# Where three groups of transfers stand in a decoder trunk on one core: the sums of the down weights in gate and up, the loads at the border, the transposes of the last product

## The chip, the cores and the metric

The kernel runs on one core of a Trainium2 chip. Its metric is the time of one execution on the device in microseconds, taken as the median of several runs. TensorE (PE in the rows; PEld is its weight load) multiplies, VectorE (DVE), ScalarE (ACT) and GpSimd (POOL) work on elements, and SyncE (SP) issues most of the transfers, which 16 DMA engines carry out. SP and POOL each feed a queue of their own to the same 16 engines.

## The reference

The program is a decoder trunk of two layers on 1024 tokens of width 1024, all in float32.

```python
for i in range(DEPTH):                       # DEPTH = 2
    h = rmsnorm(x, norm_mix[i])
    x = x + (even_mixer(...) if i % 2 == 0 else odd_mixer(...))
    h = rmsnorm(x, norm_ffn[i])
    x = x + conv_ffn(h, w_gate[i], w_up[i], conv_w[i], conv_b[i], w_down[i])
    gate = jax.nn.sigmoid(rmsnorm(x, norm_ple[i]) @ w_ple_gate[i])
    x = x + gate * (p[i] @ w_ple_proj[i])

def conv_ffn(h, w_gate, w_up, conv_w, conv_b, w_down):
    g = causal_dwconv(h @ w_gate, conv_w, conv_b)
    return (jax.nn.gelu(g) * (h @ w_up)) @ w_down     # D_FF = 2816
```

The even mixer projects h to queries, keys and values of two groups of heads; in one group each query keeps the 256 keys with the highest score of an indexer. The odd mixer is a dilated window attention.

## The kernel before

**Stages.** Each layer is a row of stages, and each stage has an instruction list of its own for every engine: input projection, attention, output projection, gate and up with the down pass (`ffn_stage`), and the gated embedding. Every float32 factor is split in a high and a low part (`w_hi`, `w_lo`), and a product is three matmuls (`mm3`, lines 78 to 80): ScalarE rounds the high part, GpSimd or VectorE subtracts it for the low part, and TensorE multiplies.

**Input projection of layer 0** (`project_select_stage`, names `l0in_` and `l0h_`). Six strips of 512 columns, each of 8 token tiles. While TensorE is in strip s, four chunks (512 KB each) of strip s + 1 are loaded by SP into `l0h_raw` (L1987), split by ScalarE (L2021) and by GpSimd (L2080). In ScalarE's list chunk c stands ahead of the two token tiles 2c and 2c + 1 that it copies out of PSUM, and SP stores these two tiles ahead of its next load. All along VectorE finds each query's threshold by 31 rounds of bisection (L2162 to L2172) and then makes the mask tile by tile (L2182 to L2189); ScalarE's count for the first of these tiles (L2050) stands in its list behind its work on the next-to-last strip. Layer 1 has the simpler `projection_stage` (`l1in_`, `k_raw`, `k_w_lo`).

**The sums.** The down projection is done by seven products of half size (`DOWN`), r = 0 to 6; three of them (r = 2, 3, 6) have a sum of two blocks of `w_down` on the right. Class `RightSums` makes these sums in device memory, by transfers alone: six copies of 1408 KB (`copy`, L2263), then six transfers of the same size that add onto what is there (`add`, L2269). They are issued by GpSimd, and the program before has them in the input projection of each layer: copies beside strips 1 and 2, adding transfers beside strips 3 and 4.

**Gate and up** (`ffn_stage`, names `l0ff_`, `l1ff_`). NG = 11 groups of W = 14 steps; a step is 12 matmuls on one of 14 factors of a group, with `q` the number of the step over all groups and `n` its number in the group. The weights of a group come in two loads of 1024 KB, `raw_g` and `raw_u` (L830), which SP issues at n = 8 and 9 once the buffers' last use is over; a ring of six slots `w_hi`, `w_lo` holds split factors ahead of TensorE. `Q` is the number of all steps.

**Down pass.** Seven products of 11 steps each, z = 11r + k. A step multiplies a left factor (from `a11`, `a12`, `a22`, read back from `acts`, in the rows `l0ff_a`) with a right one (`d_one`, and for a difference `d_two`), both split three steps ahead: `split_right` and `split_left` on ScalarE, `sum_left`, `sum_right`, `low_right`, `low_left` on VectorE. `load_down(z)` loads the right factor. In step z VectorE also adds one tile of the product before to `x` (`add`, L2804), which is reloaded from `kept`. During the last product `nfeed.turn` transposes the first two normed token tiles of the next stage (L188) in banks of `bank_u`; product 5 stands in these banks until VectorE has added it. Turn 0 takes banks 0 and 1, turn 1 banks 2 and 3, and product 5's eight adds go through banks 0 to 3 twice.

## Time and profile before

| | |
|---|---|
| median of 3 runs | 3159.48 us (3158.32 to 3169.77) |
| the profiled execution, its own time | 3161.22 us |
| its span in the profile | 3159.2 us |
| TensorE busy | 3014.0 us, 95% of the span |
| VectorE busy | 2271.2 us, 72% |
| ScalarE, GpSimd busy | 1444.3 us (46%), 1403.9 us (44%) |
| mean DMA rate | 110 GB/s |

The difference of 2.0 us between time and span lies ahead of and behind the profiled instructions. Layer 0's input projection lies at 226 to 517 us of the span, its gate and up at 945 to 1355, its down pass at 1355 to 1591; the stages of layer 1 that the text speaks of are at 1714 to 1990, 2392 to 2802 and 2802 to 3037. TensorE's clock is given as a share of its full 2.4 GHz: 1.00 is that, 0.50 is 1.2 GHz.

### The profile page before, as it was taken

The page shows a single profiled execution, that of the slowest core. Times are in us where ns is not written, and L with a number is a line of the kernel's source. Part 1 is how long each engine was busy: PE and PEld are TensorE (multiplying, and loading weights), DVE is VectorE, ACT ScalarE, POOL GpSimd, SP SyncE. Part 2 cuts the span into 40 slices and gives each one's busy share as a digit, 9 for nine tenths or more (in the row PEclk, how much of TensorE's full clock was granted, in tenths as well). Part 3 has the DMA queues.
Part 4 walks back from the last instruction along what each step waited for, and adds up shares of the span by engine and source line. Part 5 has one row for each costly group of instructions (what it writes and reads, how often), then busy time and mean ns, then how long its engine had stood idle before and what let it go on. Part 6 is the DMA issues. An engine that isn't in the chain of part 4 may idle for free. (4 is left out here: it accounts for less than half of the span.)

```text
span 3159.2 us, 44227 instructions
## 1 busy us (share of the span) xinstructions
PE 3014.0 (95%) x14830; PEld 2520.0 (80%) x14830; DVE 2271.2 (72%) x3459; ACT 1444.3 (46%) x3125; POOL 1403.9 (44%) x905
## 2 busy tenths in 40 slices
PE   7999889999999999999899999999998999999989
PEld 6777777989877888878788788899886888878877
DVE  6599957879458887779943332799648888779952
ACT  4384435878343343334432211688633333434431
POOL 3105445366235655523422455677315566533330
PEclk9999999999999999999999999999999999999999
DMA  5325574223312222365311585323121222265411
GB/s 179 122 61 164 140 181 122 60 54 78 116 54 80 80 84 82 127 246 193 99 61 37 195 178 170 81 66 80 54 88 54 96 82 80 81 240 197 157 48 53
DMA packets 288086, 349.07 MB, mean 110 GB/s; under 512 B 88316, under 2 KB 181292, under 8 KB 287916
## 3 DMA queue, kind: packets, MB, share of 16 engines
q1 hardware_dynamic: 274860, 312.27, 30.9%
q0 software_dynamic: 13056, 34.60, 4.9%
q8 instruction: 98, 1.61, 0.2%
q14 instruction: 72, 0.59, 0.1%
HBM read 268.70 MB, written 112.20 MB: 121 GB/s over the span
## 5 line engine op out<-in xcount | busy, mean ns | idle before, releaser
L2162 DVE TENSOR_SCALAR_CACHE_REDUCE k_x<-k_x,l0in_cand,l0in_want 128x384 bf16<-128x384 f32 (+1 forms) x186 | 175.0, 1004 | 1.2 <-DVE l0in_before L2157 0.2
L78 PE MATMUL l1in_acc<-k_w_lo,k_hi 128*128 128x512 f32 x384 | 151.7, 395 | 5.2 <-POOL k_w_lo L681 2.7
L2648 POOL TENSOR_TENSOR l1ff_w_lo<-l1ff_raw_g,l1ff_w_hi 128x512 fp32r<-128x512 f32 x64 | 93.5, 1466 | 138.6 <-ACT l1ff_w_hi L2511 138.5
L2648 POOL TENSOR_TENSOR l0ff_w_lo<-l0ff_raw_g,l0ff_w_hi 128x512 fp32r<-128x512 f32 x64 | 91.9, 1438 | 140.8 <-ACT l0ff_w_hi L2511 140.7
L2540 ACT ACTIVATE k_x<-k_x 128x512 f32<-128x512 f32 x88 | 55.7, 633 | 212.3 <-DVE k_x L2742 212.3
L79 PE MATMUL l1in_acc<-k_w_hi,k_lo 128*128 128x512 f32 x384 | 150.8, 393 | 0.0
L80 PE MATMUL l1in_acc<-k_w_hi,k_hi 128*128 128x512 f32 x384 | 150.6, 392 | 0.0
L725 DVE TENSOR_TENSOR l1in_sq<-l1in_out 128x512 f32<-128x512 f32 x32 | 40.4, 1264 | 114.7 <-ACT l1in_out L658 114.0
L1619 DVE TENSOR_TENSOR l1dil_pt_lo<-l1dil_ring,l1dil_pt_hi 128x512 fp32r<-128x512 f32 x192 | 101.9, 553 | 4.6 <-ACT l1dil_pt_hi L1555 2.3
L1635 DVE CUSTOM_DVE_ANT_0 l1dil_s<-l1dil_s,l1mix_sliding 128x128 f32<-128x128 f32 (+7 forms) x128 | 97.3, 761 | 9.0 <-PE l1dil_s L1719 4.7
L1555 ACT ACTIVATE l1dil_pt_hi<-l1dil_ring 128x512 fp32r<-128x512 f32 x192 | 92.5, 492 | 22.6 <-PE l1dil_ring L1702 21.4
L2652 POOL TENSOR_TENSOR l0ff_s_lo<-l0ff_s_tmp,l0ff_s_hi 128x512 fp32r<-128x512 f32 x31 | 47.8, 1543 | 101.2 <-ACT l0ff_s_hi L2557 101.2
L2652 POOL TENSOR_TENSOR l1ff_s_lo<-l1ff_s_tmp,l1ff_s_hi 128x512 fp32r<-128x512 f32 x31 | 48.0, 1551 | 99.7 <-ACT l1ff_s_hi L2557 99.7
L78 PEld LDWEIGHTS l1in_acc<-k_w_lo,k_hi 128*128 128x128 f32 x384 | 72.7, 189 | 21.4 <-POOL k_w_lo L681 3.6
L681 POOL TENSOR_TENSOR k_w_lo<-k_raw,k_w_hi 128x1024 fp32r<-128x1024 f32 x20 | 48.7, 2435 | 87.3 <-ACT k_w_hi L646 87.3
L1896 DVE SCALAR_TENSOR_TENSOR k_x<-l0h_r,l0h_wi,k_x 128x384 f32<-128x384 f32 (+2 forms) x96 | 83.2, 957 | 5.8 <-ACT l0h_r L1881 5.8
L80 PEld LDWEIGHTS l1in_acc<-k_w_hi,k_hi 128*128 128x128 f32 x384 | 72.9, 190 | 15.5
L79 PEld LDWEIGHTS l1in_acc<-k_w_hi,k_lo 128*128 128x128 f32 x384 | 73.0, 190 | 14.9
L2790 DVE TENSOR_TENSOR l0ff_d_lo<-l0ff_d_one,l0ff_d_hi 128x512 fp32r<-128x512 f32 x77 | 66.5, 864 | 18.4 <-ACT l0ff_d_hi L2566 18.3
L2790 DVE TENSOR_TENSOR l1ff_d_lo<-l1ff_d_one,l1ff_d_hi 128x512 fp32r<-128x512 f32 x77 | 66.3, 862 | 17.8 <-ACT l1ff_d_hi L2566 17.4
L2698 DVE TENSOR_TENSOR l1ff_w_lo<-l1ff_raw_u,l1ff_w_hi 128x512 fp32r<-128x512 f32 x65 | 52.4, 806 | 35.8 <-ACT l1ff_w_hi L2511 35.8
L2566 ACT ACTIVATE l1ff_d_hi<-l1ff_d_one 128x512 fp32r<-128x512 f32 x77 | 48.1, 625 | 65.2 <-DVE l1ff_d_one L2786 38.6
(647 smaller groups left out, 11304.4 us busy)
## 6 DMA issues: line engine op xcount, KB each, us to landing
l_right_sums<-in_w_down POOLq DMA_DIRECT2D x24, 1408.0 KB, 14.0
acts<-k_x SPq DMA_DIRECT2D x88, 256.0 KB, 2.0
k_raw<-in_w_in_odd SPq DMA_DIRECT2D x24, 512.0 KB, 4.9
l0ff_raw_g<-in_w_gate SPq DMA_DIRECT2D x11, 1024.0 KB, 5.2
l0ff_raw_u<-in_w_up SPq DMA_DIRECT2D x11, 1024.0 KB, 5.6
l0ff_a<-acts SPq DMA_DIRECT2D x44, 256.0 KB, 5.3
l0ff_d_one<-in_w_down SPq DMA_DIRECT2D x44, 256.0 KB, 2.8
l1ff_raw_g<-in_w_gate SPq DMA_DIRECT2D x11, 1024.0 KB, 5.2
```

The lines of the kernel that those rows point to most:

```text
L78: pe.matmul(out, a_hi, b_lo, start=start, stop=False)
L79: pe.matmul(out, a_lo, b_hi, start=False, stop=False)
L80: return pe.matmul(out, a_hi, b_hi, start=False, stop=stop)
L1555: act.activation(pt_hi[:, slot, c:512], ring[:, bank, c:512], ACT.Copy).then_inc(rounded, 1)
L1619: dve.tensor_tensor(pt_lo[:, slot, c:512], ring[:, bank, c:512], pt_hi[:, slot, c:512].bitcast(F32), ALU.subtract).then_inc(drained, 1)
L1635: dve.tensor_tensor_reduce(s, s, crow[:, b, 0:(t + 1) * P] if FOX else masks[t], -SCALE, 1e38, ALU.add, ALU.min, nmax[:, i:i + 1]).then_in ...
L1896: dve.scalar_tensor_tensor(cols, r[:, (t - T0) % NB, 0:(t + 1) * P], wi[:, t, bass.ds(h, 1)], cols, ALU.mult, ALU.add).then_inc(acc_done, 1)
L2162: tick(dve.tensor_scalar(hits[:, cols], score[:, cols], cand[:, i:i + 1].bitcast(F32), want[:, i:i + 1], ALU.is_ge, ALU.add, accum_out=exc ...
L2540: act.activation(a[n % 2], c[n % 2], ACT.Gelu_apprx_tanh).then_inc(gelu_done, 1)
L2648: pool.tensor_tensor(buf.ring_lo[q % R][:], operand(q), buf.ring_hi[q % R][:].bitcast(F32), ALU.subtract).then_inc(w_lo_done[0], 1)
L2652: pool.tensor_tensor(s_lo[z % DEEP][:], left(z), s_hi[z % DEEP][:].bitcast(F32), ALU.subtract).then_inc(s_lo_done[0], 1)
L2790: dve.tensor_tensor(d_lo[z % DEEP][:], d_raw[z % DEEP][0][:], d_hi[z % DEEP][:].bitcast(F32), ALU.subtract).then_inc(d_lo_done, 1)
```

## The change

Three edits, each in both layers.

1. The six copies and six adding transfers leave the input projections. They are issued by GpSimd in gate and up, one at n = 6 and one at n = 13: the copies in groups 0 to 2, the adding ones in groups 3 to 5.
2. At the border from gate and up to the down pass, SP's list has another order. Four loads of `a11` and `a12` go out at step Q - 1, ahead of the last stores; the right factor z = 7 goes ahead of the remaining ones; the loads of `a22` and of `x` follow one at a time behind the right factors z = 8 to 20.
3. `nfeed.turn` stands behind steps 7 and 9 of the last product instead of 6 and 8. The first turn waits for all but two of product 5's adds, the second one for all.

```diff
@@ projection_stage, gpsimd
-                    if s in (1, 2) and c < right_sums.count // 2:
-                        right_sums.copy(pool, (s - 1) * (right_sums.count // 2) + c)
-                    if s in (3, 4) and c < right_sums.count // 2:
-                        right_sums.add(pool, (s - 3) * (right_sums.count // 2) + c)
@@ project_select_stage, gpsimd
-                    if s == 1 and t < right_sums.count:
-                        right_sums.copy(pool, t)
-                    if s == 3 and t < right_sums.count:
-                        right_sums.add(pool, t)
@@ ffn_stage, sync, in the loop over q
+                if q == Q - 1:
+                    sp.wait_ge(filled, Q - 2)
+                    load_part(a11, (0, 0), range(8, 11), a11_in)
+                    load_part(a12, (0, 1), range(8, 9), a12_in[1])
@@ ffn_stage, sync, behind that loop
-            sp.wait_ge(filled, Q - 2)
-            load_part(a11, (0, 0), range(8, 11), a11_in)
-            load_part(a12, (0, 1), range(8, 9), a12_in[1])
-            sp.wait_ge(stored[0], 16 * 2 * NG)
-            load_part(a12, (0, 1), range(9, 11), a12_in[2])
-            sp.wait_ge(filled, Q)
-            load_part(a22, (1, 1), range(4, 8), a22_in)
-            sp.wait_ge(stored[1], 16 * 2 * NG)
             for z in range(DEEP + 3, Z):
                 r, k = divmod(z, KB2)
                 load_down(z)
-                if (r, k) in ((0, 7), (0, 9)):
-                    t = k - 7
-                    for u in (t, t + 1):
-                        sp.dma_start(x[:, u, :], buf.kept[u * P:(u + 1) * P, :]).then_inc(x_in[0], 16)
-                if (r, k) == (0, 10):
-                    load_part(a22, (1, 1), range(8, 11), a22_in)
-                if r == 1 and k in (1, 4, 6, 8):
-                    t = {1: 4, 4: 5, 6: 6, 8: 7}[k]
-                    sp.dma_start(x[:, t, :], buf.kept[t * P:(t + 1) * P, :]).then_inc(x_in[1], 16)
+                if (r, k) == (0, 7):
+                    sp.wait_ge(stored[0], 16 * 2 * NG)
+                    load_part(a12, (0, 1), range(9, 11), a12_in[2])
+                    sp.wait_ge(stored[1], 16 * 2 * NG)
+                    sp.wait_ge(filled, Q)
+                if 8 <= z <= 11 or z in (14, 16, 18, 20):
+                    t = z - 8 if z <= 11 else z // 2 - 3
+                    sp.dma_start(x[:, t, :], buf.kept[t * P:(t + 1) * P, :]).then_inc(x_in[t // 4], 16)
+                if 9 <= z <= 11 or z in (13, 15, 17, 19):
+                    i = z - 5 if z <= 11 else z // 2 + 1
+                    load_part(a22, (1, 1), range(i, i + 1), a22_in)
@@ ffn_stage, gpsimd
+                if n in (6, 13) and grp < 6:
+                    i = 2 * (grp % 3) + (n == 13)
+                    right_sums.copy(pool, i) if grp < 3 else right_sums.add(pool, i)
@@ ffn_stage, tensor, down(z)
-                if r == len(DOWN) - 1 and k in (6, 8):
-                    if k == 6:
-                        pe.wait_ge(added, ADDED[r])
-                    nfeed.turn(pe, (k - 6) // 2)
+                if r == len(DOWN) - 1 and k in (7, 9):
+                    pe.wait_ge(added, ADDED[r] - 2 if k == 7 else ADDED[r])
+                    nfeed.turn(pe, (k - 7) // 2)
```

GpSimd's list in layer 0's input projection, beside strip 1, had these rows before: the low part of a chunk, two copies, the work on the statistics of two token tiles, and the next chunk.

```order
L2080 TENSOR_TENSOR l0h_w_lo<-l0h_raw,l0h_w_hi 128x1024
L2263 DMA l_right_sums<-in_w_down 704x512 x2
L2085 TENSOR_SCALAR k_stats<-k_stats 128x2x8
L2087 TENSOR_TENSOR k_stats<-k_stats,l0in_half 128x2x8
L2080 TENSOR_TENSOR l0h_w_lo<-l0h_raw,l0h_w_hi 128x1024
```

GpSimd's list of the changed kernel, in the first group of gate and up from n = 5 on (low parts for the ring, sums of weights, copies; its lines are numbered some 10 lower):

```order
L2638 TENSOR_TENSOR l0ff_w_lo_8910<-l0ff_raw_g,l0ff_w_hi_8904 128x512
L2255 DMA l_right_sums<-in_w_down 704x512
L2638 TENSOR_TENSOR l0ff_w_lo_8906<-l0ff_raw_g,l0ff_w_hi_8900 128x512
L2638 TENSOR_TENSOR l0ff_w_lo_8908<-l0ff_raw_g,l0ff_w_hi_8902 128x512
L2638 TENSOR_TENSOR l0ff_w_lo_8910<-l0ff_raw_g,l0ff_w_hi_8904 128x512
L2623 TENSOR_TENSOR k_x<-l0ff_raw_g 128x512
L2623 TENSOR_TENSOR k_x<-l0ff_raw_u 128x512
L2638 TENSOR_TENSOR l0ff_w_lo_8906<-k_x,l0ff_w_hi_8900 128x512
L2626 TENSOR_TENSOR l0ff_raw_g<-l0ff_raw_g 128x4x128
L2255 DMA l_right_sums<-in_w_down 704x512
```

A copy now stands between two low parts, the second of which is the last use of `raw_g` in the group, and another one among the sums for the next group.

SP's list at the border before, from the last store of gate and up on: ten loads of left factors stand ahead of the right factor of z = 7 (the row of L2278).

```order
L2413 DMA acts<-k_x 128x512
L2423 DMA l0ff_a_9895<-acts 128x512
L2423 DMA l0ff_a_9896<-acts 128x512
L2423 DMA l0ff_a_9897<-acts 128x512
L2423 DMA l0ff_a_9906<-acts 128x512
L2423 DMA l0ff_a_9907<-acts 128x512
L2423 DMA l0ff_a_9908<-acts 128x512
L2423 DMA l0ff_a_9913<-acts 128x512
L2423 DMA l0ff_a_9914<-acts 128x512
L2423 DMA l0ff_a_9915<-acts 128x512
L2423 DMA l0ff_a_9916<-acts 128x512
L2278 DMA l0ff_d_one_9880<-in_w_down 128x512
```

The same place of the changed kernel, from the last store on:

```order
L2405 DMA acts<-k_x 128x512
L2270 DMA l0ff_d_one_9862<-in_w_down 128x512
L2415 DMA l0ff_a_9889<-acts 128x512
L2415 DMA l0ff_a_9890<-acts 128x512
L2270 DMA l0ff_d_one_9859<-in_w_down 128x512
L2471 DMA k_x<-kept 128x1024
L2270 DMA l0ff_d_one_9860<-in_w_down 128x512
L2471 DMA k_x<-kept 128x1024
L2415 DMA l0ff_a_9895<-acts 128x512
L2270 DMA l0ff_d_one_9861<-in_w_down 128x512
L2471 DMA k_x<-kept 128x1024
L2415 DMA l0ff_a_9896<-acts 128x512
```

The right factor of z = 7 is now first behind the store, and those of z = 8, 9 and 10 each have a load of `x` or two behind them.

TensorE's list at the first turn before: the last matmuls of step 6 (slot 9873 of the right factor), the transposes, the first matmuls of step 7 (slot 9874).

```order
L80 MATMUL l0ff_bank_g<-l0ff_d_hi_9869,l0ff_s_hi_9861 128x512
L188 MATMUL l0ff_bank_u<-k_square,l0pg_xn 128x128 x8
L78 MATMUL l0ff_bank_g<-l0ff_d_lo_9874,l0ff_s_hi_9862 128x512
L79 MATMUL l0ff_bank_g<-l0ff_d_hi_9870,l0ff_s_lo_9866 128x512
L80 MATMUL l0ff_bank_g<-l0ff_d_hi_9870,l0ff_s_hi_9862 128x512
```

The same turn in the changed kernel, between steps 7 and 8, so one step (12 matmuls) later:

```order
L80 MATMUL l0ff_bank_g<-l0ff_d_hi_9852,l0ff_s_hi_9844 128x512
L188 MATMUL l0ff_bank_u<-k_square,l0pg_xn 128x128 x8
L78 MATMUL l0ff_bank_g<-l0ff_d_lo_9857,l0ff_s_hi_9845 128x512
L79 MATMUL l0ff_bank_g<-l0ff_d_hi_9853,l0ff_s_lo_9849 128x512
L80 MATMUL l0ff_bank_g<-l0ff_d_hi_9853,l0ff_s_hi_9845 128x512
```

The transposes are the same eight matmuls; only their place has moved.

## Rows read from the trace of the kernel before

**Rows 1.** The page, part 1: busy time, share of the span, instructions
```profile
PE 3014.0 (95%) x14830; PEld 2520.0 (80%) x14830; DVE 2271.2 (72%) x3459; ACT 1444.3 (46%) x3125; POOL 1403.9 (44%) x905
```

**Rows 2.** TensorE's waits, whole span: for whom, us in total, times, longest
```profile
PE l0w_t L78 <- POOL l0h_w_lo L2080: 18.5, 2, 13.3
...
PE l0ff_bank_u L188 <- DVE k_x L2804: 8.5, 1, 8.5
PE l1ff_bank_u L188 <- DVE k_x L2804: 8.1, 1, 8.1
PE l0ff_bank_g L78 <- DVE l0ff_s_lo L2808: 5.5, 1, 5.5
PE l1ff_bank_g L78 <- DVE l1ff_s_lo L2808: 5.4, 1, 5.4
...
PE l0w_t L78 <- POOL l0in_w_lo L2080: 4.2, 1, 4.2
...
PE l1in_acc L78 <- POOL k_w_lo L681: 2.7, 1, 2.7
```

**Rows 3.** Landing of the loads into l0h_raw (L1987), layer 0's input projection
```profile
DMA to landing us min/median/max: 3.6/4.9/13.5
```

**Rows 4.** Windows: PE, PEld, DVE, ACT, POOL busy; granted clock, DMA share, GB/s
```profile
333.00:376.00 43.00, 43.00 (x191) 35.52 (x190) 42.27 (x99) 22.41 (x142) 22.09 (x12) 1.00 0.33 98
416.00:428.00 12.00, 6.79 (x20) 5.10 (x19) 11.90 (x23) 5.32 (x35) 5.45 (x3) 0.72 1.12 231
468.00:480.00 12.00, 7.77 (x23) 5.82 (x22) 6.46 (x9) 5.20 (x11) 6.40 (x4) 0.72 0.29 115
```

**Rows 5.** Timeline of PE, 326 to 333 us: start, length, [wait before it]
```profile
326.88 0.80 PE L78 MATMUL l0w_t<-l0h_w_lo,l0h_hi 128*128 128x512 f32 x1 [13.27 <-POOL l0h_w_lo L2080]
...
332.16 0.45 PE L78 MATMUL l0w_t<-l0h_w_lo,l0h_hi 128*128 128x512 f32 x1
```

**Rows 6.** Timeline of DVE, 440 to 513 us: the mask tiles
```profile
473.32 0.15 DVE L2186 TENSOR_SCALAR l0in_cnt<-l0in_cnt 128x1 f32<-128x1 f32 x1 [31.34 <-ACT k_x L2050]
...
511.45 1.23 DVE L2189 SCALAR_TENSOR_TENSOR k_x<-k_x 128x1024 f32<-128x1024 f32 x1
```

**Rows 7.** GpSimd's DMA queue, 270 to 330 us: packets, MB, share of 16 engines
```profile
q0 software_dynamic: 2208, 8.65, 46.8%
```

**Rows 8.** The same queue, 375 to 440 us
```profile
q0 software_dynamic: 4320, 8.65, 75.1%
```

**Rows 9.** Line L2269, adding transfers: time to issue on POOL, ns min/median/max
```profile
L2269 POOL DMA_DIRECT2D l_right_sums<-in_w_down x12: 1105/1183/1607, 378.4 to 1895.6; - x12
```

**Rows 10.** Timelines of SP, ACT and PE around one group of gate and up
```profile
1034.69 0.38 SPq L830 DMA_DIRECT2D l0ff_raw_g<-in_w_gate  x1
...
1041.11 0.63 ACT L2511 ACTIVATE l0ff_w_hi<-l0ff_raw_g 128x512 fp32r<-128x512 f32 x1 [6.59 <-DMA l0ff_raw_g<-in_w_gate]
...
1055.39 0.39 PE L78 MATMUL l0ff_bank_g<-l0ff_lo,l0ff_w_hi 128*128 128x512 f32 x1
```

**Rows 11.** Timelines of SP, ACT and PE at the border of layer 0
```profile
1368.04 4.79 SPq L2423 DMA_DIRECT2D l0ff_a<-acts  x10
1372.93 0.49 SPq L2278 DMA_DIRECT2D l0ff_d_one<-in_w_down  x1
...
1379.84 0.63 ACT L2566 ACTIVATE l0ff_d_hi<-l0ff_d_one 128x512 fp32r<-128x512 f32 x1 [9.72 <-DMA l0ff_d_one<-in_w_down]
...
1381.89 0.77 PE L78 MATMUL l0ff_bank_g<-l0ff_d_lo,l0ff_s_hi 128*128 128x512 f32 x1 [5.52 <-DVE l0ff_s_lo L2808]
```

**Rows 12.** A window at that border, columns as in rows 4
```profile
1376.30:1387.10 10.80, 5.28 (x14) 4.14 (x14) 5.15 (x7) 3.56 (x7) 1.27 (x1) 0.68 1.04 403
```

**Rows 13.** Timelines of DVE and PE in layer 0's last product
```profile
1569.63 0.68 DVE L2804 TENSOR_TENSOR k_x<-k_x,l0ff_bank_u 128x512 f32<-128x512 f32 x1
...
1573.96 1.97 PE L188 MATMUL l0ff_bank_u<-k_square,l0pg_xn 128*128 128x128 f32 x8 [8.53 <-DVE k_x L2804]
1575.58 0.78 PE L78 MATMUL l0ff_bank_g<-l0ff_d_lo,l0ff_s_hi 128*128 128x512 f32 x1
```

More of the change, by code:

```diff
@@ L582, in load, with projection_stage @@
                      .rearrange("(k p) n -> p k n", p=P)).then_inc(arrived, 16)
-def projection_stage(nc, name, right_sums, x, buf, ident, proj, vsplit, vstored, stats, next_head=None):
+def projection_stage(nc, name, x, buf, ident, proj, vsplit, vstored, stats, next_head=None):
     S = len(buf.strips)
@@ L1930, in _, with project_select_stage @@
             first.begin(pe, hi, lo)
-def project_select_stage(nc, name, right_sums, hi, lo, strips, proj, vsplit, vstored, room, stats, score, mask, tail, square, decay, first, next_head=None):
+def project_select_stage(nc, name, hi, lo, strips, proj, vsplit, vstored, room, stats, score, mask, tail, square, decay, first, next_head=None):
     S = len(strips)
@@ L3006, in trunk @@
                                           EXTRA_AT + 9 * KB)
-                            project_select_stage(nc, L + "in", right_sums[layer], hi, lo, [w[:, c:c + 512] for c in HEADS_SRC], proj, vsplit, vstored, room, stats,
+                            project_select_stage(nc, L + "in", hi, lo, [w[:, c:c + 512] for c in HEADS_SRC], proj, vsplit, vstored, room, stats,
                                                  score, mask, tail, square, decay, first, fox)
@@ L3011, in trunk @@
                                   second_at=MERGED_AT + 8 * KB)
-                    projection_stage(nc, L + "in", right_sums[layer], x, heads, ident, proj, vsplit, vstored, stats, dil)
+                    projection_stage(nc, L + "in", x, heads, ident, proj, vsplit, vstored, stats, dil)
                 recycle(nc)
```

## The prediction

> **What bounds the kernel now.** I read the busy times first: TensorE works through 95% of the span [rows 1], and the change leaves its matmuls alone. So only its waits can be won or lost, and the list of waits comes next [rows 2]. The reader is to see three places. In layer 0's input projection TensorE waits 18.5 us in two pieces for low parts that GpSimd makes, and 4.2 us once more in a later strip (layer 1: 2.7). At each border to the down pass it waits 5.5 and 5.4 us for `s_lo`. At the first transposes of the next stage it waits 8.5 and 8.1 us for VectorE's last add of product 5. These waits sum to 52.9 us. Then I read timelines around each place for what was late, and windows for the granted clock, because a wait has a second price: after the 13.27 us wait at 326.88 the next 12 matmuls take 332.16 - 326.88 = 5.28 us [rows 5], where 12 of the clean window take 12 x 43.00 / 191 = 2.70 us [rows 4]. I count 2.6 us of slow clock behind a long wait. The windows behind the other waits of the stage stand at 0.72 [rows 4], so each of them has such a tail.
>
> **Edit 1, what it removes.** Beside copies and adding transfers a chunk's load takes up to 13.5 us to land, against a median of 4.9 and a best of 3.6 [rows 3]. In the clean window TensorE is busy in all of its 43.00 us at a DMA share of 0.33 [rows 4]: without transfers this stage has no wait of its own. So both waits for `l0h_w_lo` go, the 4.2 us one of the later strip too, since the same chain of load, split and low part stands behind it. That is 18.5 + 4.2 = 22.7 us, and three tails of 2.6 make 7.8: 30.5 us. VectorE could take the bound instead. It stands idle for 31.34 us before 473.32, waiting for ScalarE's count, which is queued behind ScalarE's copies out of PSUM and so moves forward with TensorE; then it works without a pause to 511.45 + 1.23 = 512.68 [rows 6]. If ScalarE comes 30.5 us earlier, the idle time is used up to the last microsecond, and VectorE ends at 512.7 - 30.5 = 482, about level with TensorE. I take 30; the bounds are 15 (VectorE or ScalarE keeps half of it) and 31. Layer 1 gives 2.7 us and a shorter tail: the wait is a fifth of the long one, and I take 1.7 us, so 4.4 (bounds 0 and 5.3).
>
> **Edit 1, what it adds.** The same twelve transfers per layer move the same bytes in another stage. Their cost for the 16 engines: six copies take 46.8% of 60 us, 4.7 us each [rows 7]; six adding ones 75.1% of 65 us, 8.1 us each [rows 8]. GpSimd is held 1.1 to 1.6 us for the issue of one [rows 9]. I do not have the copies' issue in a row and take the same for them. In gate and up the thing that can be late is the next group's weights. In one group `raw_g` is issued at 1034.69, ScalarE splits it at 1041.11, having waited 6.59 us for it, and TensorE uses it first at 1055.39 [rows 10]. From a split to the matmul the border takes 1381.89 - 1379.84 = 2.05 us [rows 11], so the factor is ready at 1043.2, 12.2 us early. That is the cover. The transfer at n = 6 is issued two to three steps, of 2.7 us, ahead of these loads, so it meets them; the one at n = 13 is done long before the next ones. Delay, worked out in two ways: the adding transfer's whole 8.1 us and its issue of 1.6 us, 9.7 us; or the worst stretching of rows 3, 13.5 / 4.9 = 2.8 times the 6.4 us of landing here, 11.3 us more. Both stay under 12.2, so I take nothing lost in gate and up. The margin of the second is small, and if the cover is gone, each of the 12 meetings (six groups, two layers) costs its excess and a tail of 2.6. A gain is excluded: TensorE does not wait there now.
>
> The Trainium skill, "DMA: Bandwidth & Descriptors", section "Queues, rings and completion order", has each DMA engine take its queues in turn, packet by packet. By that rule a load beside one transfer lasts at most about twice as long, some 6.4 us more, and the sum is the same. Rows 3 stretch further than that, with several transfers in flight. The same skill, "SBUF — State Buffer", section "SBUF: two separate sides", speaks against the change: VectorE in its fast modes can keep GpSimd from writing descriptors. That would hold GpSimd's low parts as well. The issue times of rows 9 show no hold beyond 1.6 us, and half of them were measured with VectorE all but saturated, as it is in the clean window (42.27 of 43.00 us [rows 4]); should the hold be longer in gate and up, it would act as the first rival below does.
>
> **Edit 2.** The first matmul of the down pass waits for the right factor of z = 7: its load is issued at 1372.93, behind ten loads that take the queue from 1368.04 for 4.79 us, ScalarE splits it at 1379.84, and TensorE goes on at 1381.89 after 5.52 us [rows 11]. In the new order it is issued at about 1368.1. With the same 6.9 us to its split it comes at 1375.0, and TensorE could go at 1377.0; it is ready at 1381.89 - 5.52 = 1376.4. So 0 to 0.7 us are left. Gain per layer: 5.5 and a tail of 2.6, less up to 0.7, so 7.5; two layers 15 (bounds 5 and 16). The four loads moved ahead of the stores go out in the last step of gate and up; SP has nothing else to send between them. What is late next is product 1's loads: each step now moves a right pair of 512 KB with 512 KB of `x` or 256 KB of `a22`, on average 896 KB (917,500 bytes) in 2.7 us, 340 GB/s. The border itself moved 403 GB/s at a share of 1.04 [rows 12]. It fits, with a sixth to spare.
>
> **Edit 3.** The first turn stood behind step 6, whose matmuls ended at 1573.96 - 8.53 = 1565.43, and waited until 1573.96 for the last of product 5's eight adds. The sixth, the last one that it will wait for now, ends at 1569.63 + 0.68 = 1570.3 [rows 13]. The turn also stands a step later: TensorE ends step 7 at 1565.4 + 2.7 = 1568.15 and waits until 1570.3, 2.15 us. Behind step 9, at 1573.6 + 2.0 or later, the second turn finds all adds done or misses them by a little. Before, 8.53 us and a tail of some 2 us were lost (one matmul takes 0.78 us behind the turn [rows 13], where one in the clean flow of rows 10 takes 0.39). After, 2.15 and a tail of at most 1.7. Gain 7.5 us in layer 0 and 7 in layer 1, 14.5 (bounds 8 and 19). The norm of the other token tiles and the next stage's start keep their place.
>
> **The sum.** 30 + 4.4 + 15 + 14.5 = 63.9 us. From the profiled execution's own 3161.2 us that is 3097.3; this execution is 1.7 us above the median of the three runs, less than the sum is worth. I say 3097.
>
> **The rivals.**
> *The transfers hold gate and up's weights back (the other side).* Place: the loads of `raw_g` and `raw_u` in groups 0 to 5. For it: the 13.5 us landing, and a load here is twice a chunk. Against it: only one transfer is in flight at n = 6, not several. It decides from 63.9 / 12 = 5.3 us lost at each meeting, 2.7 of wait and 2.6 of tail, so from a delay of 12.2 + 2.7 = 14.9 us. With a delay of 20 us it costs (7.8 + 2.6) x 12 = 125 us: 3222. In a mild form (delays of 13 to 14 us at the six adding meetings) it costs 6 x 4 = 24: 3121. Chance 0.04 for the strong form, 0.10 for the mild.
> *VectorE or ScalarE becomes the bound of the select stage.* For it: the idle 31.34 us are exactly what the gain uses, and VectorE works through all of the 39 us behind. Then edit 1 gives 15 instead of 30: 3112. Chance 0.12.
> *The border's stall comes back in product 1.* For it: the share of 1.04, with loads of `x` in between the right factors. Edit 2 then gives 5 instead of 15: 3107. Chance 0.11. To this belongs that the order at the border does nothing, since z = 7 lands late with its neighbours whatever stands ahead: also near 3107.
> My forecast, 3085 to 3104, has the remaining 0.63.
>
> **How the numbers follow.** A measurement of this kernel tells 0.5%, 15.8 us, from no change. The forecast and the second and third rival are all faster by more than that, as is most of the mild form: 0.91. Its rest and cases between the mild and the strong form give 0.05 for the same, the strong form 0.04 for slower. All terms at their upper bounds give 31 + 5 + 16 + 19 = 71 us, 3090, and half as much again as the tails I count (six of 2.6) could be hidden in rows that I did not sum, so the range begins at 3083. It ends at 3124, just beyond the mild form at 3121; outside lie the strong form and mixtures of two rivals.
>
> **What the changed profile would show.** Edit 1: no waits of `l0w_t` for `l0h_w_lo`, landings of `l0h_raw` under 7 us, the stage over at about 487 instead of 517, `right_sums` rows in gate and up, landings of `raw_g` longer at groups 0 to 5 and TensorE without a wait there. Wrong, if L78 or L80 wait for `l0ff_w_lo` or `w_hi` in these groups, or if the stage ends with VectorE alone at work. Edit 2: `d_one` of z = 7 issued right behind the last store, the wait under 1 us; wrong, if waits for `d_lo` or `s_lo` stand in product 1. Edit 3: the turn's wait at 2 us; wrong, if a second one stands at the next turn.

## The result and the profile after

The changed kernel takes 3167.74 us (median of 20 runs, 3161.39 to 3172.52), the kernel before 3157.74 us (20 runs beside them): ratio 1.0029, 95% interval 1.0022 to 1.0037. The forecast was 3097 us with a range of 3083 to 3124. The time lies outside it and is slightly longer than before.

TensorE's work is the same ([rows 1] for before); the page of the changed kernel:

```profile
PE 3018.5 (95%) x14830; PEld 2517.2 (79%) x14830; DVE 2285.1 (72%) x3459; ACT 1438.9 (45%) x3125; POOL 1385.1 (44%) x905
```

Its list of TensorE's waits answers to [rows 2]. Every wait that was to go is gone. `l0w_t` no longer waits for `l0h_w_lo`, the border's wait for `s_lo` is no longer near 5 us, and the turn's is 2.0 us in both layers (one sign of edit 2 being wrong shows faintly: a wait of 1.9 us for a left factor's low part, `s_lo` by GpSimd, in layer 1's product 1). In their place stand waits of gate and up, for low parts made by VectorE (L2691) and by GpSimd (L2638):

```profile
PE l0ff_bank_u L78 <- DVE l0ff_w_lo L2691: 20.1, 6, 4.2
PE l1ff_bank_u L78 <- DVE l1ff_w_lo L2691: 17.6, 6, 4.2
...
PE l0ff_bank_g L78 <- POOL l0ff_w_lo L2638: 6.5, 3, 2.9
...
PE l1ff_bank_g L78 <- POOL l1ff_w_lo L2638: 4.7, 3, 2.8
```

To see where the time is, I laid the first and last starts of each stage's matmuls side by side. One pair of rows for layer 0's gate and up, the kernel before and then the changed one (durations in ns, then first and last start in us):

```profile
L78 PE MATMUL l0ff_bank_g<-l0ff_lo,l0ff_w_hi x176: 389/389/775, 916.3 to 1345.7; 128*128 128x512 f32 x176
L78 PE MATMUL l0ff_bank_u<-l0ff_t_lo,l0ff_w_hi x132: 389/389/527, 947.6 to 1353.9; 128*128 128x512 f32 x132
```

```profile
L78 PE MATMUL l0ff_bank_g<-l0ff_lo,l0ff_w_hi x176: 389/389/775, 881.4 to 1346.9; 128*128 128x512 f32 x176
L78 PE MATMUL l0ff_bank_u<-l0ff_t_lo,l0ff_w_hi x132: 389/389/515, 912.8 to 1355.1; 128*128 128x512 f32 x132
```

The stage begins 34.9 us earlier and ends 1.2 us later. (Its first matmul is at 916.3 in the kernel before, not at the 945 given for this stage further up; in layer 1 it is at 2363.6. All distances here count from there.) The whole account in one profiled execution of each (us):

| stage | predicted | measured |
|---|---|---|
| input projection, layer 0 | -30 | -32.0 |
| input projection, layer 1 | -4.4 | -4.6 |
| border and turn, layers 0 and 1 | -29.5 | -12.4 and -6.6 |
| gate and up, layers 0 and 1 | 0 | +36.0 and +32.0 |
| elsewhere | 0 | -3.8 |
| span | -63.9 | +8.6 |

The windows say the same from the other side: mean clock and DMA share of gate and up in both layers, before and then after (columns as in [rows 4]). The DMA share rises from 0.26 to 0.42, and the stretch is longer by 36 and 31 us for the same matmuls.

```profile
916.00:1355.00 439.00, 427.46 (x1864) 352.04 (x1863) 354.10 (x379) 171.68 (x276) 252.48 (x168) 0.98 0.26 89
2363.00:2802.00 439.00, 427.40 (x1866) 352.32 (x1865) 357.11 (x379) 170.65 (x276) 255.71 (x168) 0.98 0.26 89
```

```profile
881.00:1356.00 475.00, 438.12 (x1864) 357.30 (x1862) 363.96 (x379) 168.45 (x276) 254.79 (x180) 0.96 0.42 121
2347.00:2817.00 470.00, 438.84 (x1859) 357.98 (x1857) 362.00 (x375) 166.43 (x273) 254.43 (x179) 0.96 0.42 122
```

**Two things happen in a group with transfers.** First, at n = 6. The timelines of GpSimd, SP, ScalarE and TensorE in layer 0's fifth group of the changed kernel:

```profile
1094.05 1.10 POOL L2261 DMA_DIRECT2D l_right_sums<-in_w_down  x1
...
1096.49 0.38 SPq L826 DMA_DIRECT2D l0ff_raw_g<-in_w_gate  x1
...
1109.14 0.63 ACT L2501 ACTIVATE l0ff_w_hi<-l0ff_raw_g 128x512 fp32r<-128x512 f32 x1 [14.84 <-DMA l0ff_raw_g<-in_w_gate]
...
1111.16 0.50 PE L78 MATMUL l0ff_bank_g<-l0ff_lo,l0ff_w_hi 128*128 128x512 f32 x1 [2.08 <-POOL l0ff_w_lo L2638]
```

The load is issued 2.4 us behind the adding transfer and takes 12.7 us to its split; in the kernel before it takes 5.1 to 5.4, and 6.4 once in each layer. In group 0 the transfer goes out 6.7 us ahead of the load, which then takes 5.7 us: so each layer has five meetings of a transfer with the loads, two with a copy and three with an adding transfer, not six. TensorE uses the factor as soon as it is ready, 2.08 us late. Second, at n = 13, the same group, GpSimd, VectorE and TensorE:

```profile
1122.57 1.11 POOL L2261 DMA_DIRECT2D l_right_sums<-in_w_down  x1
1123.29 1.71 POOL L2630 TENSOR_TENSOR l0ff_raw_g<-k_x,l0ff_raw_g 128x512 f32<-128x512 f32 x1
...
1127.00 1.64 POOL L2630 TENSOR_TENSOR l0ff_raw_u<-k_x,l0ff_raw_u 128x512 f32<-128x512 f32 x1
...
1123.10 6.11 DVE L2691 TENSOR_TENSOR l0ff_w_lo<-k_x,l0ff_w_hi 128x512 fp32r<-128x512 f32 x1
...
1129.26 0.50 PE L78 MATMUL l0ff_bank_u<-l0ff_lo,l0ff_w_hi 128*128 128x512 f32 x1 [4.18 <-DVE l0ff_w_lo L2691]
```

The same place of the kernel before, GpSimd and VectorE:

```profile
1129.03 1.62 POOL L2640 TENSOR_TENSOR l0ff_raw_g<-k_x,l0ff_raw_g 128x512 f32<-128x512 f32 x1
1130.62 1.74 POOL L2636 TENSOR_TENSOR l0ff_raw_u<-l0ff_raw_u 128x512 f32<-128x512 f32 x1
...
1129.42 1.78 DVE L2698 TENSOR_TENSOR l0ff_w_lo<-k_x,l0ff_w_hi 128x512 fp32r<-128x512 f32 x1
```

VectorE's subtraction takes 6.11 us instead of 1.78 and ends half a microsecond behind the last of the four GpSimd operations that follow the issue (1127.00 + 1.64 = 1128.64). It takes 5.7 us in the three groups with copies, 6.1 in those with adding transfers, in both layers.

### The profile page after: what moved, and what is told of

It is laid out like the page before. It is cut to its first block and busy times, and to the rows that moved or that the text cites. A ratio compares the mean times of both kernels' runs of the same rounds, so it can differ in the third digit from the quotient of the medians.

```text
span 3167.8 us, 44229 instructions
## 1 busy us (share of the span) xinstructions
PE 3018.5 (95%) x14830; PEld 2517.2 (79%) x14830; DVE 2285.1 (72%) x3459; ACT 1438.9 (45%) x3125; POOL 1385.1 (44%) x905
## 5 line engine op out<-in xcount | busy, mean ns | idle before, releaser
L2638 POOL TENSOR_TENSOR l0ff_w_lo<-l0ff_raw_g,l0ff_w_hi 128x512 fp32r<-128x512 f32 x64 | 91.9, 1439 | 177.6 <-ACT l0ff_w_hi L2501 177.5
L2638 POOL TENSOR_TENSOR l1ff_w_lo<-l1ff_raw_g,l1ff_w_hi 128x512 fp32r<-128x512 f32 x64 | 92.3, 1446 | 175.2 <-ACT l1ff_w_hi L2501 175.0
L2691 DVE TENSOR_TENSOR l0ff_w_lo<-l0ff_raw_u,l0ff_w_hi 128x512 fp32r<-128x512 f32 x65 | 52.4, 806 | 78.6 <-ACT l0ff_w_hi L2501 78.6
L2691 DVE TENSOR_TENSOR l1ff_w_lo<-l1ff_raw_u,l1ff_w_hi 128x512 fp32r<-128x512 f32 x65 | 52.4, 806 | 76.9 <-ACT l1ff_w_hi L2501 76.9
L1551 ACT ACTIVATE l1dil_pt_hi<-l1dil_ring 128x512 fp32r<-128x512 f32 x192 | 92.4, 492 | 22.7 <-PE l1dil_ring L1698 21.4
L78 PE MATMUL l0ff_bank_u<-l0ff_lo,l0ff_w_hi 128*128 128x512 f32 x176 | 72.6, 413 | 20.8 <-DVE l0ff_w_lo L2691 20.1
L78 PE MATMUL l1ff_bank_u<-l1ff_lo,l1ff_w_hi 128*128 128x512 f32 x176 | 73.4, 417 | 18.3 <-DVE l1ff_w_lo L2691 17.6
L2501 ACT ACTIVATE l0ff_w_hi<-l0ff_raw_g 128x512 fp32r<-128x512 f32 x64 | 39.7, 621 | 103.9 <-DMA l0ff_raw_g<-in_w_gate 98.5
L2501 ACT ACTIVATE l1ff_w_hi<-l1ff_raw_g 128x512 fp32r<-128x512 f32 x64 | 39.7, 620 | 101.7 <-DMA l1ff_raw_g<-in_w_gate 97.1
```

The source lines that it names most:

```text
L78: pe.matmul(out, a_hi, b_lo, start=start, stop=False)
L1551: act.activation(pt_hi[:, slot, c:512], ring[:, bank, c:512], ACT.Copy).then_inc(rounded, 1)
L2501: act.activation(buf.ring_hi[q % R][:], operand(q), ACT.Copy).then_inc(w_hi_done, 1)
L2638: pool.tensor_tensor(buf.ring_lo[q % R][:], operand(q), buf.ring_hi[q % R][:].bitcast(F32), ALU.subtract).then_inc(w_lo_done[0], 1)
L2691: dve.tensor_tensor(buf.ring_lo[q % R][:], operand(q), buf.ring_hi[q % R][:].bitcast(F32), ALU.subtract).then_inc(w_lo_done[1], 1)
```

## The experiments

All ratios are to the kernel before, run beside them on the same chip; intervals are of 95%. Gate and up of a kernel is the distance from its first to its last matmul there, layer 0 / layer 1 (before: 438.1 / 438.0; changed kernel: 474.1 / 470.0).

**1. The transfers back in the input projections, edits 2 and 3 kept.**

```diff
-                if n in (6, 13) and grp < 6:
-                    i = 2 * (grp % 3) + (n == 13)
-                    right_sums.copy(pool, i) if grp < 3 else right_sums.add(pool, i)
```

(and the calls in the two input projections as before)

> The transfers of the sums stand in the input projections again; the border and the turns keep the new order. If gate and up lose their 68 us in the changed kernel (36.0 in layer 0, 32.0 in layer 1) to the transfers alone, both stages take their old time here, the down passes stay 12.4 and 6.6 us shorter, and the kernel takes about 3158 - 19 = 3139 us, a ratio of 0.994. If the new order of loads at the border or the turns have a part in the loss, gate and up or the stages behind stay longer and the ratio is above 0.997.

Measured: 3124.4 us, ratio 0.9906 (0.9888 to 0.9925), gate and up 436.9 / 438.2. The loss is the transfers' alone. The down passes are 15.5 and 13.5 us shorter than before, more than the 12.4 and 6.6 that I read from the changed kernel and took into this expectation (10 of the 15 us by which it is too high): these are the 29 us that the prediction had for edits 2 and 3.

**2. n = 13 moved to n = 1 of the next group.**

```diff
-                if n in (6, 13) and grp < 6:
+                g = grp - (n == 1)
+                if n in (6, 1) and 0 <= g < 6:
```

> The second transfer of a group is issued at n = 1 of the next group, behind GpSimd's run of sums of weights, instead of n = 13, in the middle of it. Theory 1: VectorE's low part of a sum, which takes 5.7 to 6.1 us instead of 1.78 in the groups with transfers, is held because the issue brings GpSimd's run and this one operation of VectorE out of step. Then it takes 1.8 us again in all groups, TensorE's ten waits on it (34.9 us in both layers) go with their slow clock behind (about 1.4 us each), and the kernel takes about 49 us less than the changed one: 3118, ratio 0.987. Theory 2: the bytes of the transfers, beside the stores and loads of gate and up, are what costs. Then the same bytes cost the same at n = 1, closer to the loads of n = 8: ratio 1.003 or more. The waits for the low parts of raw_g (11.2 us) stay in both.

Measured: 3153.4 us, ratio 0.9992 (0.9983 to 1.0001), gate and up 464.8 / 461.6. VectorE's operation takes 1.78 us in all 22 groups, so its hold does come from the place of the issue. But 49 us were expected back and 14 came (12 by the ratios), since the waits for `raw_g` grew:

```profile
PE l0ff_bank_g L78 <- POOL l0ff_w_lo L2638: 17.4, 4, 7.2
...
PE l1ff_bank_g L78 <- POOL l1ff_w_lo L2638: 13.8, 4, 4.6
```

**3. n = 6 moved to n = 10.**

```diff
-                if n in (6, 13) and grp < 6:
+                if n in (10, 13) and grp < 6:
```

> The first transfer of a group is issued at n = 10, when the next group's weights have landed, instead of n = 6, just ahead of their loads; the second stays at n = 13. If the transfer ahead of the loads stretches them (landing of raw_g 12.7 us where 5.2 is usual), the landings are short again, the waits for the low parts of raw_g (11.2 us in both layers, and about 8 us of slow clock behind them) go, and 19 us are saved of the changed kernel: 3148, ratio 0.997. VectorE's held operation at n = 13 stays at 5.7 to 6.1 us, and its waits stay. If the load's delay comes from something else (SP's queue, late freeing of the buffer), nothing changes: 1.003.

Measured: 3107.7 us, ratio 0.9849 (0.983 to 0.9868), gate and up 440.7 / 441.9. My split of the 68 us (49 for the hold, 19 for the load) was wrong. This one move brings back 61.5 of them. VectorE is still held, up to 6.2 us in six groups of each layer,

```profile
L2691 DVE TENSOR_TENSOR l0ff_w_lo<-k_x,l0ff_w_hi x11: 1769/5746/6187, 900.8 to 1292.4; 128x512 fp32r<-128x512 f32 x11
```

but TensorE hardly waits for it (4.8 and 4.1 us in all): the ring of split factors is full enough to cover most of the 4 us by which the operation is longer.

**4. Both moved.**

```diff
-                if n in (6, 13) and grp < 6:
+                g = grp - (n == 1)
+                if n in (10, 1) and 0 <= g < 6:
```

> Both transfers of a group are moved, to n = 10 and to n = 1 of the next group. If the two costs are separate and these are all, gate and up take their old time in both layers (about 440 us), and the whole gain of the changed kernel elsewhere, 55 to 60 us, is kept: 3099, ratio 0.981. If a transfer costs something wherever it stands in gate and up, the ratio stays above 0.985, and the waits of TensorE in this stage show where.

Measured: 3095.2 us, ratio 0.9812 (0.9796 to 0.9829), gate and up 437.1 / 438.0. This is the lowest median of all (experiments 7 and 8 are within its interval), and nothing is paid for the same 24 transfers. The issue lines of the changed kernel's page and of this one (the last number is the median landing in us):

```profile
l0ff_raw_g<-in_w_gate SPq DMA_DIRECT2D x11, 1024.0 KB, 7.6
...
l0ff_raw_g<-in_w_gate SPq DMA_DIRECT2D x11, 1024.0 KB, 5.4
```

**5. n = 6 moved to n = 3**, the second at n = 13.

```diff
-                if n in (6, 13) and grp < 6:
+                if n in (3, 13) and grp < 6:
```

> As the changed kernel, with the first transfer of a group at n = 3 instead of n = 6; the second stays at n = 13. Theory 1, the transfer is costly because the loads of the next weights (issued at n = 8) land behind it: at n = 3 it has 14 us of its own ahead of these loads, the landings of raw_g stay under 8 us, and the kernel comes out like the one with the transfer at n = 10: 3108, ratio 0.985. Theory 2, its place ahead of the last low parts of a group on GpSimd is what delays the loads (they are issued 3.6 us later than before, seen from TensorE's steps): n = 3 is ahead of them too, so most of the loss stays, ratio 1.000 or above.

Measured: 3134.9 us, ratio 0.9941 (0.9929 to 0.9953), gate and up 454.8 / 456.6. Between the theories. The transfer went out 7 us ahead of the loads, not the 14 that I had taken, and an adding one lands 12 to 14 us behind its issue, so it still overlaps them. `raw_g` takes 6.1 to 9.3 us instead of up to 13.7 and is waited for no more (0.2 us once), yet 12.8 us in each layer are waited for VectorE's held operation. I read this so: a load that is only 1 to 4 us late is enough to leave the ring too empty to cover the hold.

**6. Both transfers of a group at n = 6.**

```diff
-                if n in (6, 13) and grp < 6:
-                    i = 2 * (grp % 3) + (n == 13)
-                    right_sums.copy(pool, i) if grp < 3 else right_sums.add(pool, i)
+                if n == 6 and grp < 6:
+                    for i in (2 * (grp % 3), 2 * (grp % 3) + 1):
+                        right_sums.copy(pool, i) if grp < 3 else right_sums.add(pool, i)
```

> Both transfers of a group at n = 6, none at n = 13 (no held operation of VectorE). The landing of raw_g should be its own 5.2 us and the two transfers' engine time ahead of it: 5.2 + 2 x 8.1 = 21.4 us in the adding groups, 5.2 + 2 x 4.7 = 14.6 in the copying ones. If the cover is 6.8 us (TensorE's first use at 1049.95 against factors ready at 1043.2 in the kernel before), that is a wait of about 8 us in three groups and of 1 us in three, with 2.6 and 1.4 us of slow clock behind: some 40 us per layer over the kernel with n = 1 and n = 10, 3177, ratio 1.006. If the cover is the 12.2 us of the prediction, the excess is 2.8 us in three groups: some 16 us per layer, 3127, ratio 0.991.

Measured: 3222.1 us, ratio 1.021 (1.0196 to 1.0224), gate and up 499.1 / 496.7. Landings of 13.4 to 15.1 us with two copies and 18.5 to 20.3 with two adding transfers, near the 14.6 and 21.4 expected (13.2, 13.6 and 18.1 to 18.7 in layer 1; 10.8 and 11.5 behind group 0's copies, where nothing is waited for): a load lasts about its own time and the transfers' engine time, or somewhat less. The waits are 5.0 to 7.6 and 10.7 to 12.7 us, above even the smaller cover's 1 and 8, and the kernel is 45 us above this expectation:

```profile
1116.35 0.38 SPq L826 DMA_DIRECT2D l0ff_raw_g<-in_w_gate  x1
...
1134.89 0.63 ACT L2501 ACTIVATE l0ff_w_hi<-l0ff_raw_g 128x512 fp32r<-128x512 f32 x1 [21.87 <-DMA l0ff_raw_g<-in_w_gate]
...
1136.91 0.80 PE L78 MATMUL l0ff_bank_g<-l0ff_lo,l0ff_w_hi 128*128 128x512 f32 x1 [10.65 <-POOL l0ff_w_lo L2638]
```

The factor was wanted at 1136.91 - 10.65 = 1126.26, 9.9 us behind the issue of its load; in the kernel before this distance is 14.4 to 16.8 us. The cover itself had shrunk.

**7. Issues without bytes.** The kernel of experiment 4, with a transfer of one row at n = 6 and at n = 13 beside the others.

```diff
+                if n in (6, 13) and grp < 6:
+                    right_sums.tiny(pool, 2 * grp + (n == 13))
+    def tiny(self, pool, i):
+        pool.dma_start(self.rest[i:i + 1], self.blocks[(0, 0)][i:i + 1]).then_inc(self.moved, 16)
```

> The kernel with the transfers at n = 1 and n = 10, and beside them a transfer of one row (2 KB) at n = 6 and one at n = 13 in the same six groups: the issue by GpSimd without the bytes. If the issue alone holds VectorE's low part at n = 13, this operation takes over 5 us there again instead of 1.78; landings of raw_g stay at 5.4 us, and the time rises by at most 10 us (TensorE waits little for the held operation while the ring is full): 3095 to 3105, ratio 0.981 to 0.984. If the bytes or the number of descriptors hold it, it stays at 1.78 us, and the time at 3095.

Measured: 3098.8 us, ratio 0.9825 (0.9813 to 0.9838), gate and up 437.0 / 437.1. An issue at n = 6 without the bytes costs nothing: `raw_g` lands in 5.2 to 5.5 us (6.4 once). So what stretches the load there is the bytes. The hold is back, with 2 KB, in three of six groups (5.6 us each), and the operation takes 1.85 us in the other three. In both layers the held ones are groups 3 to 5, where the issue takes 0.53 us and not 0.50. Held, GpSimd and VectorE:

```profile
1097.62 0.53 POOL L2249 DMA_DIRECT2D l_rest<-in_w_down  x1
1098.17 1.31 POOL L2635 TENSOR_TENSOR l0ff_raw_g<-k_x,l0ff_raw_g 128x512 f32<-128x512 f32 x1
...
1098.15 5.64 DVE L2699 TENSOR_TENSOR l0ff_w_lo<-k_x,l0ff_w_hi 128x512 fp32r<-128x512 f32 x1
```

and not held, in another group:

```profile
1021.91 1.30 POOL L2635 TENSOR_TENSOR l0ff_raw_g<-k_x,l0ff_raw_g 128x512 f32<-128x512 f32 x1
...
1021.91 1.86 DVE L2699 TENSOR_TENSOR l0ff_w_lo<-k_x,l0ff_w_hi 128x512 fp32r<-128x512 f32 x1
```

Bytes are not needed for the hold. What separates the cases is who starts first behind the issue. In all 42 held ones (12 each in the changed kernel and experiments 3 and 5, 6 here) VectorE's row starts 0.02 to 0.21 us ahead of GpSimd's next one; in the 6 cases here that are not held, GpSimd's starts with it or 0.01 us ahead, and without an issue, as in the kernel before, 0.4 to 0.5 us ahead.

**8. The transfer of n = 13 one operation earlier**, ahead of the first sum; the other at n = 10.

```diff
                 if q + L < Q and (q + L) % 2 == 0:
                     low(q + L)
+                if n in (10, 13) and grp < 6:
+                    i = 2 * (grp % 3) + (n == 13)
+                    right_sums.copy(pool, i) if grp < 3 else right_sums.add(pool, i)
                 if n in (11, 12) and grp + 1 < NG:
```

> As the kernel with n = 10 and n = 13, but at n = 13 the transfer is issued one operation earlier in GpSimd's list: behind the low part and ahead of the first sum, where VectorE's operation on the sum does not stand beside it yet. If the hold comes from VectorE's operation starting while the issue goes on, it is gone (1.8 us in all groups), and the remaining waits on it (8.9 us in both layers) as well: 3097, ratio 0.981. If any issue inside GpSimd's run of operations gives the run right of way until its end, the operation is held as long as before or longer (6 to 7 us), and the time stays at 3108 or above.

Measured: 3099.2 us, ratio 0.9817 (0.9803 to 0.9831), gate and up 436.9 / 437.1. The operation takes 1.76 to 1.78 us in every group, and GpSimd's operation beside it starts 0.40 us ahead again. One place in GpSimd's list makes or removes the hold.

**9. n = 6 in every other group only.** The kernel of experiment 4, with n = 6 for n = 10 in groups 0, 2 and 4.

```diff
-                if n in (10, 1) and 0 <= g < 6:
+                if n in (10 if grp % 2 else 6, 1) and 0 <= g < 6:
```

> The kernel with the transfers at n = 1 and n = 10 (3095), but in groups 0, 2 and 4 the first transfer stands at n = 6 again. With all six at n = 6 the kernel took 3153, so the six meetings with the loads cost 58 us in the two layers. If each meeting costs by itself, half of them cost 29 us: 3124, ratio 0.990. If a meeting eats TensorE's lead (the ring of split factors), so that the next group's loads go out later and meet the next transfer with less cover, then a group without a meeting in between restores the lead, and three single meetings cost next to nothing: 3095 to 3103, ratio 0.981 to 0.983, no wait over 2 us for a low part of raw_g.

Measured: 3116.1 us, ratio 0.9878 (0.9862 to 0.9893), gate and up 443.4 / 442.6. This costs 6.3 and 4.6 us in gate and up, where n = 6 in all groups (experiment 2 against 4) costs 27.7 and 23.6. That looks like far less than half, but it isn't half of the same thing: of the five real meetings two are left, one with a copy (group 2, landings of 9.4 and 9.0 us, nothing waited for) and one of the three with an adding transfer (group 4). If the cost went with the adding meetings alone and each cost by itself, a third would be 9.2 and 7.9 us. So no more than 3 us per layer are left for a lead that is eaten from meeting to meeting. Nor does a group without a meeting restore the lead: in layer 0 the issue of `raw_g` stands 14.8 us ahead of its use at group 2's copy, then 11.7 us, 12.1 at group 4's adding transfer, then 10.3 and 11.1. The group with the adding transfer waits 3.1 and 3.4 us:

```profile
1079.22 0.38 SPq L826 DMA_DIRECT2D l0ff_raw_g<-in_w_gate  x1
...
1094.36 0.50 PE L78 MATMUL l0ff_bank_g<-l0ff_lo,l0ff_w_hi 128*128 128x512 f32 x1 [3.05 <-POOL l0ff_w_lo L2638]
```

Both theories miss: the single meeting costs, against the second, and less than 29 us in gate and up (10.9), against the first. The rest of the 21 us over experiment 4 lies mostly in the down pass, with a wait of 3.9 and 4.3 us at its first matmul (below).

**10. and 11. Edits 2 and 3 each alone** on the kernel before (the diffs are the pieces of the change under `ffn_stage, sync` and `down(z)`).

> The kernel before with the new order of loads at the border alone. Prediction's term: 15 us in both layers, ratio 0.9953; the wait for s_lo of 5.5 and 5.4 us is gone. The rival of a stall that comes back in product 1: 5 us, 0.998, with waits for the right factors or left factors there.

> The kernel before with the turns two places later alone (behind steps 7 and 9). Prediction's term: 14.5 us in both layers, ratio 0.9954; the wait at the first turn is 2 us instead of 8.5 and 8.1. If the adds of product 5 are then late for the second turn, a wait stands there and the gain is under 8 us.

Measured: border alone 3142.6 us, ratio 0.9956 (0.9943 to 0.997); turn alone 3140.1 us, 0.9958 (0.9945 to 0.9972). By the ratios that is 13.9 and 13.2 us of the 15 and 14.5 predicted (by the medians 11.8 and 14.3; the intervals leave 4 us either way). The wait for `s_lo` at the border is gone in the first, and the turn waits 1.7 and 2.0 us in the second.

## Why the prediction was wrong

**Where it was right.** Edit 1's gain: 32.0 and 4.6 us in the two profiled executions, against 30 and 4.4. Part of that is the one execution of the kernel before: with the transfers still in the input projections, experiments 1, 10 and 11 have this gain at 28 to 30 us in layer 0 and at 0 to 1.3 in layer 1, and experiments 1 and 4, alike in all but the place of the transfers, differ by 29 us. That is inside the bounds (15 to 36), and 5 us below what was said. The landings of `l0h_raw` (L1983 now) are 4.8 us at most, and VectorE, idle before for 31.34 us [rows 6], waits for ScalarE's counts half a microsecond at most and ends at 480.2. So the rival of VectorE as the bound did not come true; stage and VectorE end almost level, as worked out. Edits 2 and 3 are worth about what was said, alone (27 us) and together (30 us in experiment 1). The turn waits 2.00 us where 2.15 were expected:

```profile
1565.75 1.09 PE L188 MATMUL l0ff_bank_u<-k_square,l0pg_xn 128*128 128x128 f32 x8 [2.00 <-DVE k_x L2797]
```

With all of this and nothing lost in gate and up the forecast was 3097; experiment 4, where gate and up really loses nothing, takes 3095. That the two are so close is in part luck: the gain there is 60 us of the 63.9, and the forecast started from an execution 6 us above the median that the kernel before has beside experiment 4.

**The step that failed** is the cover in gate and up, "12.2 us early". The delay beside it was sound: 9.7 us as one bound, 12.7 - 5.2 = 7.5 measured. The cover was wrong twice.

First, a misread row. I took 1055.39 in [rows 10] for TensorE's first use of the group's `raw_g`. TensorE's row for this use is 5.4 us earlier, at the change from the last `t_lo` step of a group to the first `lo` step of the next:

```profile
1049.72 0.39 PE L80 MATMUL l0ff_bank_u<-l0ff_t_hi,l0ff_w_hi 128*128 128x512 f32 x1
1049.95 0.39 PE L78 MATMUL l0ff_bank_g<-l0ff_lo,l0ff_w_hi 128*128 128x512 f32 x1
```

The factor is ready at 1043.2, so the cover was 6.8 us in that group, less than the delay. A group has 16 matmuls of this form (176 in 11 groups), and the one at 1049.95 is the first of its group; 1055.39 is two steps later. One of the matmuls of a factor at 1055.39 looks like any other: a form's name does not say which group it belongs to, so steps have to be counted from a landmark.

Second, the cover is not a constant. What counts is the distance from the issue of `raw_g` to the matmul that wants it. In layer 0's groups with adding transfers (us; the third column is landing until ScalarE's split; the wait is the third and 2.05 for the low part, less the second):

| kernel | issue to need | landing | wait |
|---|---|---|---|
| before | 15.1 to 16.8 | 5.1 to 5.4 | 0 |
| changed | 12.6 to 12.8 | 12.2 to 13.7 | 1.6 to 2.9 |
| n = 6 and 1 (2) | 9.7 to 10.2 | 11.9 to 15.0 | 4.1 to 7.2 |
| n = 10 and 13 (3) | 11.7 | 5.2 to 5.5 | 0 |
| n = 1 and 10 (4) | 13.7 to 14.7 | 5.4 to 5.5 | 0 |
| both at n = 6 (6) | 8.7 to 9.9 | 18.5 to 20.3 | 10.7 to 12.7 |

For the changed kernel's group above: 12.7 + 2.05 - 12.6 = 2.1, measured 2.08. A load that lands undisturbed, in 5.2 us, would have had a cover of 12.6 - 5.2 - 2.05 = 5.4 us there. SP may issue the load only when GpSimd has made the group's last low part. My reading is this. These run ahead of TensorE while the ring is full; once a load is late the ring empties, the last low part is late, and the next load goes out later. The lead returns slowly or hardly: in the changed kernel from 12.8 to 14.0, 14.7, 15.4 and 16.2 us in the four groups behind the last transfer, in experiment 2 from 9.8 to 10.4, 10.7, 10.3 and 10.9. So a later meeting finds less cover than the first one. A late load is not the only thing that eats it: in experiment 3 no load is late, and with the hold alone the distance falls to 11.7 us. And it varies by 1 to 2 us without any of this: in experiment 1, with no transfer in the stage, it is 13.6 to 14.9 us in the same three groups. The sum for the last column holds in every group; what sets the second column is read from the table, no experiment set the lead by itself, and experiment 9 speaks for it only weakly.

**A term that was missing** is the hold of VectorE at n = 13. I asked what the issue costs GpSimd (1.1 to 1.6 us, measured 0.7 and 1.1) and not what runs beside the place where it is put. The hold alone costs 2.6 and 3.9 us (experiment 3). The transfer at n = 6 without the hold costs 26.7 and 23.6 us over the kernel before (experiment 2). Together they cost 36.0 and 32.0, which is 6.7 and 4.5 us more than their sum; TensorE then waits 16 more times than before, 46.1 us more in all, and the remaining 21.9 us are slow clock behind, 1.4 us each, not the 2.6 that I took from waits of 13 us.

So the first rival came true in its mechanism. By its own count of 12 meetings the price is 5.7 us where 5.3 decides; the loads alone (experiment 2) would have cost 4.2 and left the kernel level with the one before, at 0.9992, and the hold made it slower. Its condition, delays above 14.9 us, was worked out with the same wrong cover; delays of 7 to 8 were enough, and its chance of 0.14 was therefore far too low.

The turn-taking of queues, from the Trainium skill, "DMA: Bandwidth & Descriptors", section "Queues, rings and completion order", would have held the load to twice its time. It took 2.3 to 2.6 times as long beside one adding transfer (12.2 to 13.7 against 5.2; 11.8 to 12.4 in layer 1), so the trace does not agree with my reading of it. Own time plus the transfer's 8.1 us, 13.3, is near; with a copy, 5.2 + 4.7 = 9.9, measured 9.2 to 10.5.

**The down pass.** In experiments 2, 3, 6 and 9 (and in layer 1 of 7 and 8) the first matmul of the down pass waits 2.9 to 6.0 us behind VectorE, which waits for a left factor's load. VectorE and TensorE in experiment 3, then VectorE in experiment 4:

```profile
1321.61 0.69 DVE L2772 TENSOR_TENSOR l0ff_s_tmp<-l0ff_a,l0ff_a 128x512 f32<-128x512 f32 x1 [5.75 <-DMA l0ff_a<-acts]
...
1327.66 0.77 PE L78 MATMUL l0ff_bank_g<-l0ff_d_lo,l0ff_s_hi 128*128 128x512 f32 x1 [4.37 <-DVE k_x L2726]
...
1312.74 0.69 DVE L2773 TENSOR_TENSOR l0ff_s_tmp<-l0ff_a,l0ff_a 128x512 f32<-128x512 f32 x1 [1.30 <-DMA l0ff_a<-acts]
```

The load takes the same time in both, 7.0 and 6.8 us. What differs is when SP issues it: the run of eleven loads to which it belongs begins 9.9 us ahead of the time at which TensorE wants its first factor in experiment 3 (1313.41 against 1327.66 - 4.37), 14.1 us in experiment 4 (1304.72 against 1318.83). These 4.2 us are nearly the whole wait. It looks like the lead once more, at the end of the stage, but this was not tried; it takes part of edit 2's gain where it occurs.

**What stays open.** In the changed kernel the down passes gave 19.0 us, where the same two edits give 29 in experiment 1. The two profiles say where the 10 us are: TensorE's waits there are 5.0 and 7.9 us instead of 3.5 and 3.7, each under 2.1 and mostly for low parts of left factors, and its matmuls are busy 1.5 and 2.6 us longer, at a mean granted clock of 0.992 and 0.985 instead of 1.00. Why these low parts are late there was not tried. Nor was it tried what sets the lead.

## What to carry to other kernels

Before moving a transfer into a stage that seems to have room, find for each load there the matmul that first wants it, by counting steps from a landmark, and subtract the transfer's whole engine time; do it again with a lead smaller by 3 to 6 us, the range seen here, since what comes late eats the lead from which the next load lives. Put such a transfer right behind the landing of a periodic load, not ahead of its issue: the same bytes cost 51 us in one place and nothing in the other. Look also at what the other engine does in the microsecond in which the issue ends.

## What the hardware showed that I had not expected

VectorE's subtraction of two SBUF tiles beside a run of GpSimd operations normally costs both some time: 1.78 us instead of 0.68 for VectorE, 1.7 instead of 1.3 for GpSimd. Behind a DMA issue inside GpSimd's run it can be held until the run ends, 5.6 to 6.2 us, while GpSimd's next operations follow each other every 1.25 us, as fast as without VectorE. A transfer of 2 KB does it as well as one of 1408 KB, in three groups of six, and with the issue one place further ahead in the list it happened in none of the 12 groups with a transfer. The Trainium skill, "SBUF — State Buffer", section "SBUF: two separate sides", says that the port pair which the two engines share is locked for a whole instruction, by whichever starts first; that fits the usual case, where GpSimd starts 0.39 us ahead and VectorE takes 1.78. It does not fit the held ones: there VectorE's row starts first, by 0.02 to 0.21 us, and it is VectorE that waits, through four instructions. No run here shows why.
